# The high part of the slabs beside the two recurrences: copied on ScalarE instead of GpSimd

## What is computed

```
p = rmsnorm(x) @ w_in                       # 40 column blocks early, 24 "side" blocks later
gated linear attention over 4 heads          # recurrence 1, on tiles of 128 frames
rq, rk = rope(r_q), rope(r_k)                # x1*cos - x2*sin, x1*sin + x2*cos
retention over 4 heads                       # recurrence 2:
    scores = (q k^T) * intra_decay
    o = scores v + (q * q_decay) state
    state = chunk_decay * state + (k * k_decay)^T v
o = head_layernorm(o) * silu(gate)
merged = sigmoid(a_gla) * (o_gla @ w_gla_out) + sigmoid(a_ret) * (o_ret @ w_ret_out)
x = x + rmsnorm(merged @ w_mix_out); then the convolutional FFN
```

## Time and profile before

| what | value |
|---|---|
| median of 3 runs | 2293.21 us (2292.55 to 2293.49) |
| the profiled execution's own time | 2293.05 us |
| its span, first to last instruction | 2291.3 us |
| busy: PE, PEld | 2254.5 us (98%), 1825.4 us (80%) |
| busy: DVE, ACT, POOL | 1194.1 us (52%), 656.7 us (29%), 1528.9 us (67%) |
| mean granted TensorE clock | 0.997 |
| recurrence 1 on TensorE | from about 673 to 1003 us |
| recurrence 2 on TensorE | from about 1003 to 1252 us |

### The profile page before, as it was taken

One profiled execution on the slowest core, in us unless ns is written; L12 is line 12 of the kernel. 1 busy time (PEld: TensorE's weight loads), 2 busy tenths in 40 slices (PEclk: granted clock), 3 DMA queues, 4 the chain that ended last, 5 costly groups with the idle time before them and its releaser, 6 DMA issues. The chain is left out here.

```text
span 2291.3 us, 26890 instructions
## 1 busy us (share of the span) xinstructions
PE 2254.5 (98%) x10174; PEld 1825.4 (80%) x10174; DVE 1194.1 (52%) x1257; ACT 656.7 (29%) x1013; POOL 1528.9 (67%) x948
## 2 busy tenths in 40 slices
PE   8999999999999999999998999999999999999998
PEld 7888888888888888876665888878778888888887
DVE  7322222235018887844445434224867777776564
ACT  4323333212112222211112211114444444443422
POOL 5787777745446555577675368871999999964452
PEclk9999999999999999999999999999999999999999
DMA  4233333334422333255556656642222222246444
GB/s 178 101 111 111 111 111 111 110 118 152 166 101 89 110 111 120 90 192 174 161 158 199 198 198 230 231 170 95 82 85 83 83 83 83 92 152 211 144 142 151
DMA packets 174710, 308.97 MB, mean 135 GB/s; under 512 B 12224, under 2 KB 90304, under 8 KB 174592
## 3 DMA queue, kind: packets, MB, share of 16 engines
q1 hardware_dynamic: 174160, 306.27, 40.2%
q10 hardware_dynamic: 432, 1.11, 0.1%
HBM read 217.16 MB, written 90.18 MB: 134 GB/s over the span
## 5 line engine op out<-in xcount | busy, mean ns | idle before, releaser
L407 PE MATMUL psum<-act_hi,w_hi 128*128 128x512 f32 x1272 | 505.6, 397 | 2.7 <-POOL w_lo L2827 1.2
L409 PE MATMUL psum<-act_hi,w_lo 128*128 128x512 f32 x1272 | 496.9, 391 | 0.0
L408 PE MATMUL psum<-act_lo,w_hi 128*128 128x512 f32 x1272 | 495.8, 390 | 0.0
L407 PEld LDWEIGHTS psum<-act_hi,w_hi 128*128 128x128 f32 x1272 | 239.3, 188 | 51.5 <-POOL w_lo L2827 2.5
L409 PEld LDWEIGHTS psum<-act_hi,w_lo 128*128 128x128 f32 x1272 | 239.0, 188 | 51.2
L408 PEld LDWEIGHTS psum<-act_lo,w_hi 128*128 128x128 f32 x1272 | 239.5, 188 | 47.2
L441 POOL TENSOR_TENSOR w_hi<-w_raw,zero_col 128x1024 fp32r<-128x1024 f32 x61 | 124.0, 2033 | 208.1 <-PE psum L409 199.2
L2869 POOL TENSOR_TENSOR w_lo<-w_raw,w_hi 128x1024 fp32r<-128x1024 f32 x44 | 110.9, 2524 | 126.1 <-ACT w_hi L2880 126.1
L1315 POOL TENSOR_TENSOR k_lev<-e_t,g_x 128x896 f32<-128x896 f32 x32 | 96.3, 3010 | 127.7 <-ACT e_t L1262 92.4
L444 POOL TENSOR_TENSOR w_lo<-w_raw,w_hi 128x1024 fp32r<-128x1024 f32 x61 | 162.4, 2662 | 4.8
L407 PE MATMUL psum<-w_hi,act_hi 128*128 128x512 f32 x416 | 162.3, 390 | 1.7 <-POOL w_lo L444 1.5
(11 more groups left out here) (279 smaller groups left out, 4717.8 us busy)
## 6 DMA issues: line engine op xcount, KB each, us to landing
w_raw<-in_w_stream SPq DMA_DIRECT2D x225, 512.0 KB, 4.0
proj_scratch<-stage SPq DMA_DIRECT2D x40, 512.0 KB, 5.2
r_x<-proj_scratch SPq DMA_DIRECT2D x64, 256.0 KB, 3.1
value_scratch<-stage SPq DMA_DIRECT2D x24, 512.0 KB, 3.4
proj_scratch<-side_out SPq DMA_DIRECT2D x48, 256.0 KB, 3.1
d_raw<-ffn_scratch SPq DMA_DIRECT2D x44, 256.0 KB, 3.6
ffn_scratch<-u_lin_v SPq DMA_DIRECT2D x20, 512.0 KB, 5.9
r_v<-value_scratch SPq DMA_DIRECT2D x32, 256.0 KB, 3.1
```

Source lines behind the costliest of these rows:

```text
L407: nc.tensor.matmul(o, s_hi, m_hi, start=start, stop=False)
L408: nc.tensor.matmul(o, s_hi, m_lo, start=False, stop=False)
L409: return nc.tensor.matmul(o, s_lo, m_hi, start=False, stop=stop)
```

## The change

The split of the 24 slabs that are made beside the two recurrences is divided between two engines. The add of zero on GpSimd that made the high part is gone. `side_slab_hi` puts a copy of the same 128 x 1024 slab on ACT, with the two waits that stood before the add; `side_slab_lo` leaves the subtraction on GpSimd, which waits for the copy through `hi_split`. In recurrence 1 ACT's copies stand behind the side eviction 4t (behind `decay(1)` in the first tile) and behind `decay(4t + 3)`. In recurrence 2 the copy stands at the end of ACT's step, in every fourth step. GpSimd's subtractions stand where the pairs stood. The slabs of all other stages are split as before.

```diff
-        def split_slab(pool, n):
+        def side_slab_hi(act, n):
 
             j = n % RING
-            pool.wait_ge(raw_in[j], 16 * (n // RING + 1 + ROW_LOADS))
-            pool.wait_ge(sem["mm_half"], 2 * n - 2 * RING + 2)
-            nc.gpsimd.tensor_tensor(w_hi[:, j, :], w_raw[:, j, :],
-                                    zero_col[:, :].to_broadcast((P, D)), ALU.add).then_inc(sem["hi_split"], 1)
+            act.wait_ge(raw_in[j], 16 * (n // RING + 1 + ROW_LOADS))
+            act.wait_ge(sem["mm_half"], 2 * n - 2 * RING + 2)
+            nc.scalar.activation(w_hi[:, j, :], w_raw[:, j, :], ACT.Copy).then_inc(sem["hi_split"], 1)
+
+        def side_slab_lo(pool, n):
+
+            j = n % RING
             pool.wait_ge(sem["hi_split"], n + 1)
             nc.gpsimd.tensor_tensor(w_lo[:, j, :], w_raw[:, j, :], w_hi[:, j, :].bitcast(F32),
                                     ALU.subtract).then_inc(sem["slab_ready"], 1)
...
                 side_evict(act, 4 * t)
                 if t:
+                    side_slab_hi(act, SL_SIDE + 2 * t + 3)
+                if t:
                     rstd(t - 1, 1)
                 else:
                     decay(4 * t + 1)
+                    side_slab_hi(act, SL_SIDE + 2 * t + 3)
                     side_evict(act, 4 * t + 1)
...
                 decay(4 * t + 3)
+                side_slab_hi(act, SL_SIDE + 2 * t + 4)
                 if t:
                     side_evict(act, 4 * t + 2)
...
                     if h == 1:
-                        split_slab(pool, SL_SIDE + 2 * t + 3)
+                        side_slab_lo(pool, SL_SIDE + 2 * t + 3)
...
                     if h == 3:
-                        split_slab(pool, SL_SIDE + 2 * t + 4)
+                        side_slab_lo(pool, SL_SIDE + 2 * t + 4)
...
                 if e % 4 == 0:
-                    split_slab(pool, SL_SIDE + 19 + e // 4)
+                    side_slab_lo(pool, SL_SIDE + 19 + e // 4)
...
                 if e < SIDE_STEPS and e % 2:
                     side_evict(act, 4 * NT + 2 + e // 2)
+                if e % 4 == 0:
+                    side_slab_hi(act, SL_SIDE + 19 + e // 4)
                 if e >= MIXED_STEP:
```

## The result

| | before | with the change |
|---|---|---|
| median of 4 runs each | 2293.35 us (2292.55 to 2294.36) | 2362.07 us (2360.23 to 2362.38) |
| span of the profiled execution | 2291.3 us | 2360.6 us |
| mean granted clock | 0.997 | 0.984 |

The kernel became slower by 3.0%: the ratio is 1.0299, with an interval of 1.0286 to 1.0312.

A forecast was written before the change was run, and what follows sets the result against it. TensorE was taken to bound both recurrences. Stalls 44.7, step 0 2.9, step 28 9.3, clock 13.8 and 0.6 sum to 71.3 us, on 2293.05 giving 2364.3 us, range 2354 to 2377.

The forecast's parts named there:

- Recurrence 1, 0 us: Recurrence 1, 16 slabs: POOL's relief lands in idle time and ACT's 1.06 us copies fit its idle time; 0 us.
- Six stalls, 7.45 us each, 44.7 in all: Recurrence 2, steps 4, 8, ..., 24: TensorE waits for the serial chain of rstd, copy, subtraction and rotation; 44.7 us.
- Step 0, 2.9 us, and 0.6 of clock: Step 0: copy behind keys(0) moves POOL's subtraction 2.94 us, TensorE's wait 2.19 becomes 5.1 us; 0.6 us more clock.
- Step 28 to the next stage, 9.3 us: Last tile: late copy delays POOL's rotations to step 31, SP's loads and the next stage by 9.3 us.
- Clock, 13.8 us for six stalls: Behind each of recurrence 2's six stalls: 2.3 us lost at lower clock, bounds 1.7 and 3.4; 13.8 us in all.
- zeros for SP's later load and for POOL's lead: Recurrence 2: SP's later slab load costs 0 us; POOL's rotations get ahead again, so a stall does not grow.
- the rival's working gave 2307: Recurrence 2: rstd served early, copy follows keys(12), stalls shrink to some 2 us in all; 2307 us, chance 0.05.
- the rival on the faster side: Between the recurrences: step 0's copy done in time, wait falls to 0.2 us, 1.7 us clock stays; 2289.4 us, chance 0.03.

The follow-up runs named there:

- that part alone: The change with ACT copies only beside recurrence 1, POOL making both parts beside recurrence 2; 2293.99 us, ratio 1.0000 to the kernel before.
- recurrence 2 alone: The change with ACT copies only beside recurrence 2, POOL making both parts beside recurrence 1; 2361.72 us, ratio 1.0297 to the kernel before.
- the copy behind the keys: The change with recurrence 2's copies directly behind the keys of the same step 4k instead of behind rstd; 2303.99 us, ratio 1.0048 to the kernel before.
- the filler: The change with 64 unused identity transposes on TensorE in steps 5, 9, ..., 25 before it waits for POOL; 2351.11 us, ratio 1.0250 to the kernel before.
- the experiment with step 0: The change with only the copy for step 0 moved to the end of recurrence 1; 2356.02 us, 6.0 us less than the change.
- first experiment: The change with recurrence 2's copies four steps earlier on ACT, step 0's behind recurrence 1's last tile; 2290.6 us, ratio 0.9988 to the kernel before.
- the three built on the same early copies: Early copies with: POOL making both parts in recurrence 1, 2290.16 us; recurrence 1's copies made twice, 2290.82; step 31's r_pt before four next-stage low parts, 2290.19.

## Why the prediction was right

The forecast was 2364.3 us, in a range of 2354 to 2377; measured are 2362.07. It was right in its mechanism, and the terms of its sum stand as follows.

- **Recurrence 1, 0 us.** Right: ratio 1.0000 with that part alone. ACT's 24 copies took 1.048 us (median) against the 1.06 priced. One thing was not as drawn: POOL waited 0.22 us for a copy once, where the working had no wait. The prediction's estimate of 1.15 us by the Trainium skill (ScalarE: Activation LUTs, § Rules for kernel authors) took a price that stands there for an ACTIVATE whose bias is a pointer operand; this copy has none, and the trace's 1.04 to 1.06 us lie below it. The measurement decides for the row. The section's advice to use VectorE for adds and multiplies does not name copies, and no run here puts the copy there.
- **Six stalls, 7.45 us each, 44.7 in all.** Measured 7.36 to 7.37 each by the steps' starts, 44.2 in all. The small rest is in the copy (1.04) and the subtraction, whose rotation followed after 2.30 us instead of 2.34. The handoff from ACT to POOL, for which no row stood, took 1124.26 - 1124.18 = 0.08 us, as taken.
- **Step 0, 2.9 us, and 0.6 of clock.** Measured 2.8 us of wait (5.00 against 2.19) and no more clock in this trace: from step 1 to step 2 it took 7.67 us after and 7.65 before. But with the same wait of 5.0 us the step took 8.48 us in recurrence 2 alone, 8.03 with the copy behind the keys and 7.84 with the filler, so 0.2 to 0.8 us more clock: the 0.6 was a fair size that this one execution did not show. (The working also has the copy end at 1005.45, where 1004.43 + 1.06 is 1005.49.)
- **Step 28 to the next stage, 9.3 us.** Measured 8.0. Up to the loads the term held: from the start of step 28 to that of step 31 TensorE took 22.80 us instead of 13.47, 9.3 us more, with nothing extra for the clock, and SP issues the loads at 1306.87 instead of 1238.12, 9.2 us more than step 28 was late (59.6). But ACT began on the first of them 4.0 us after its issue and not 5.2, which shortened the wait for `r_pt` from 5.8 to 4.5 us. I had taken this part of the chain as fixed; why the load was quicker stays open.
- **Clock, 13.8 us for six stalls.** Measured 12.8 in the table, 11 to 12.6 by the filler. The mean of 2.1 us is near the 2.3 taken, but a single stall of 7.20 us cost between 1.5 and 2.9, two of them less than the lower bound. So 1.7 and 3.4 were taken as bounds of one unknown constant, where the run shows a spread from stall to stall.

The terms alone come to 67.8 us where 71.3 were forecast, all of the 3.5 us too much. The time is only 2.2 us below the forecast, since 1.5 us or so of later waits, for which there was no term, make up for a part: that much is luck.

The zeros for SP's later load and for POOL's lead also held: no stall grew from one to the next (7.20 us each time), and the experiment with step 0 showed that the others don't depend on the first. Of the rivals, the copy behind the keys was run as a kernel of its own: 2304 us where the rival's working gave 2307. That nearness is in part luck too: the rival kept 9.3 us for the end of the recurrence, where this kernel lost 4.3, and took 0.3 us for the stall at step 5, which was 1.74. The early copy was run too: 2290.6 where the rival on the faster side gave 2289.4. At step 2 its trace is 3.8 us ahead of before, close to the 3.7 of the rival's working; between the medians some 3 us of that are left.

## What to carry to other kernels

When a step is moved from an engine that runs ahead to one that runs in step with the bottleneck, ask not whether the new engine has idle time but when in its order it reaches the step, and what the old engine has queued behind the new wait. Here ACT was idle for most of recurrence 2, and yet eight copies of 1 us cost 69 us, because each stood behind work that is in step with TensorE (seven of them behind a wait for its own late product) and in front of what TensorE needed next. The same copies one tile of heads earlier in ACT's order give back everything and some 3 us more, about 0.1%. That version and the three built on the same early copies lie between 2290.2 and 2290.8 us, which can't be told apart, and all are faster than both kernels.

## What the runs showed of the hardware that was not expected

- A wait of the same 7.20 us cost TensorE between 1.5 and 2.9 us of work at the lower clock. Against the 6.04 us that step 1 takes without a wait (first experiment), a wait of 2.19 us cost 1.6 us, and waits of 5.0 us cost 1.6, 1.8, 2.0 and 2.4 us in four kernels. The loss behind a stall is not a function of its length alone.
- The spread is not noise. Behind the six stalls TensorE lost 1.6, 2.9, 2.0, 1.5, 2.8, 2.0 us in the change, 1.5, 2.8, 1.9, 1.5, 2.8, 2.0 with only step 0 early, and 2.0, 1.5, 2.8, 2.0, 1.5, 2.8 in recurrence 2 alone: three values in turn, in the last kernel begun at another one. So it matters when a stall falls; what sets the values stays open.
- After a wait of 1.74 us (step 5, copy behind the keys) the granted clock stayed at 1.00; after one of 2.19 us (step 1 before) it was 0.57 over 4 us.
- TensorE kept its full clock through a 7.4 us wait when it ran transposes whose results nobody used, and the kernel was 11 us faster for it. It is a way to measure the clock's share in a loss, and no cure for the stall.
- ACT's copies of 128 x 1024 take 1.04 us each, but of two in a row the second starts 0.95 us behind the first.
